# Two of the four weight sums of a seven-product pair formed by an accumulating DMA, with the signs moved to the token side

## The reference

```python
def rms_norm(x, g):
    xf = x.astype(F32)
    y = xf * lax.rsqrt(jnp.mean(xf * xf, axis=-1, keepdims=True) + EPS)
    return (y * g.astype(F32)).astype(x.dtype)

def swiglu(x, w_gate, w_up, w_down):
    return (jax.nn.silu(x @ w_gate) * (x @ w_up)) @ w_down

def reference(...):
    for i in range(DEPTH):            # DEPTH = 4, D_MODEL = 1024, D_FF = 2816, SEQ = 256
        x = x + 0.5 * swiglu(rms_norm(x, norm_g[i, 0]), ffn_w_gate[i, 0], ffn_w_up[i, 0], ffn_w_down[i, 0])
        ...
        x = x + mix @ w_o[i]
        x = x + 0.5 * swiglu(rms_norm(x, norm_g[i, 2]), ffn_w_gate[i, 1], ffn_w_up[i, 1], ffn_w_down[i, 1])
    return rms_norm(x, final_g)
```

## Time and profile before

| | |
|---|---|
| median of 3 runs | 1889.07 us (1888.85 to 1890.01) |
| profiled execution, first to last instruction | 1886.6 us |
| its mean granted PE clock | 0.999 |
| busy, PE / PEld / DVE / ACT / POOL | 99% / 84% / 81% / 57% / 1% |
| DMA moved | 350 MB, 186 GB/s mean |
| chunk loads, all by SP but the first | 303 into `raw`, 24 into `extra` |

### The profile page before, as it was taken

How to read it: one execution, slowest core, us unless ns; L and a number is a source line. 1 busy time by engine, 2 the same in 40 slices (tenths; PEclk the granted TensorE clock), 3 DMA queues, 4 the chain that set the end, 5 groups by cost and what they waited for, 6 DMA issues and landing times.

```text
span 1886.6 us, 22455 instructions
## 1 busy us (share of the span) xinstructions
PE 1873.3 (99%) x9364; PEld 1585.2 (84%) x9364; DVE 1531.9 (81%) x1311; ACT 1074.2 (57%) x1108; POOL 19.9 (1%) x34
## 2 busy tenths in 40 slices
PE   9999999999999999999999999999999999999998
PEld 8888998888888898788888888988888888998886
DVE  7987568987898778898789875689879987569985
ACT  6655555656565544565556554465556654556653
POOL 0000000000000000100000000000000000000000
PEclk9999999999999999999999999999999999999999
DMA  6557343456254643445625454434473545533542
GB/s 249 201 231 267 135 157 134 201 201 243 94 225 197 245 157 112 156 201 201 252 103 225 197 226 158 178 112 201 201 267 126 225 197 188 184 129 137 228 196 87
DMA packets 50052, 350.13 MB, mean 186 GB/s; under 512 B 6168, under 2 KB 6432, under 8 KB 7968
## 3 DMA queue, kind: packets, MB, share of 16 engines
q1 hardware_dynamic: 49360, 346.54, 47.5%
q10 hardware_dynamic: 592, 2.17, 0.3%
HBM read 347.63 MB, written 1.06 MB: 185 GB/s over the span
## 4 chain that ended last, share of the span: by engine, by line
PE 90%; DVE 7%; ACT 2%; issue 1%; POOL 0%; POOLq 0%; ACTq 0%; DVEq 0%
PE work L1261 18%; PE work L1263 18%; PE work L1262 18%; PE acc L1261 10%; PE acc L1263 10%; PE acc L1262 10%; DVE w_lo L756 3%; PE work L1419 1%; PE acc L1305 1%; PE work L1463 1%; PE work L1597 1%; ACT w_hi L465 1%; PE work L1563 0%; PE work L1341 0%; PE work L1567 0%
## 5 line engine op out<-in xcount | busy, mean ns | idle before, releaser
L756 DVE TENSOR_TENSOR w_lo<-raw,w_hi 128x2048 fp32r<-128x2048 f32 x327 | 741.4, 2283 | 33.5 <-ACT w_hi L465 33.4
L465 ACT ACTIVATE w_hi<-raw 128x2048 fp32r<-128x2048 f32 x327 | 613.9, 1909 | 83.2 <-DVE raw L776 64.2
L1261 PE MATMUL work<-w_hi,xg 128*128 128x512 f32 x1040 | 409.6, 394 | 1.0 <-DVE xg L1186 1.0
L1263 PE MATMUL work<-w_hi,xg 128*128 128x512 f32 x1040 | 405.5, 390 | 0.0
L1262 PE MATMUL work<-w_lo,xg 128*128 128x512 f32 x1040 | 405.0, 389 | 0.0
L1261 PE MATMUL acc<-w_hi,m_hi 128*128 128x512 f32 x824 | 325.5, 395 | 0.2
L1263 PE MATMUL acc<-w_hi,m_lo 128*128 128x512 f32 x824 | 321.2, 390 | 0.0
L1262 PE MATMUL acc<-w_lo,m_hi 128*128 128x512 f32 x824 | 320.7, 389 | 0.0
L1263 PEld LDWEIGHTS work<-w_hi,xg 128*128 128x128 f32 x1040 | 195.2, 188 | 41.1
L1261 PEld LDWEIGHTS work<-w_hi,xg 128*128 128x128 f32 x1040 | 195.3, 188 | 40.4 <-issue 1.2
L1262 PEld LDWEIGHTS work<-w_lo,xg 128*128 128x128 f32 x1040 | 195.4, 188 | 38.9
(11 more groups left out here) (200 smaller groups left out, 2169.5 us busy)
## 6 DMA issues: line engine op xcount, KB each, us to landing
raw<-stream_dram SPq DMA_DIRECT2D x303, 1024.0 KB, 5.0
extra<-stream_dram SPq DMA_DIRECT2D x24, 1024.0 KB, 6.9
x<-x_dram SPq DMA_DIRECT2D x2, 512.0 KB, 7.8
raw<-stream_dram ACTq DMA_DIRECT2D x2, 512.0 KB, 7.5
scratch<-cum_rows ACTq DMA_DIRECT2D x1, 1024.0 KB, 5.9
cst<-consts_dram SPq DMA_DIRECT2D x1, 832.0 KB, 6.4
out_dram<-x SPq DMA_DIRECT2D x3, 256.0 KB, 2.4
final_gain<-final_gain_dram SPq DMA_DIRECT2D x1, 512.0 KB, 6.9
```

What stands on the lines that cost most here:

```text
L465: nc.scalar.activation(w_hi[:, c % RING, :], raw_at(place), ACT.Copy).then_inc(hi_ready, 1)
L756: nc.vector.tensor_tensor(w_lo[:, c % RING, :], raw_at(place), w_hi[:, c % RING, :].bitcast(F32), ALU.subtract).then_inc(lo_ready, 1)
L1261: nc.tensor.matmul(dst, a_hi, b_hi, start=start, stop=False, skip_group_check=skip)
L1263: return nc.tensor.matmul(dst, a_lo, b_hi, start=False, stop=stop, skip_group_check=skip)
```

## The change

b11 is read from HBM a second time, into SUMS, behind b22. POOL, when that load has landed, issues a DMA that adds b12 from HBM onto it: SUMS then holds t1 = b11 + b12. A second DMA of POOL adds b22 from HBM onto b12's place in `raw`: t3 = b12 + b22. DVE forms t2 = b11 + t3 and t4 = b21 + t2 as before, but t2 now waits for the second of these DMAs (`t3_added`), and ACT's rounding of t1 for the first (`t1_added`). So that the products still add up, two token sums change sign (S1 = x3 - x1, and S2 and S4 follow by operations with a factor of -1), and the two hidden halves that carry the sign use a negated factor `r_neg`, one more small POOL operation for each block. Each block's six DMAs of POOL stand in POOL's list right behind that.

```diff
-FORMS = "t1", "t3", "t2", "t4"
+FORMS = "t2", "t4"
+ADDED = "t1", "t3"
...
+                loads.append(("b11", layer, n % 3, j, SUMS,
+                              ("top", no * len(PLAIN) + 1) if earlier < 0 else
+                              ("lo", c0 + order.index(("t4", SEVEN[earlier])) + 1)))
...
+            def weight_sums(no):
+
+                for p in range(no * len(SEVEN), (no + 1) * len(SEVEN)):
+                    pool.wait_ge(sums_loaded, 16 * (p + 1))
+                    pool.dma_start(raw_at(SUMS), stream[ADD_FROM[0][p]], accum_op=ALU.add).then_inc(t1_added, 16)
+                    place, count = ADD_ONTO[1][p][3:]
+                    pool.wait_ge(raw_loaded[place], 16 * count)
+                    pool.dma_start(raw_at(place), stream[ADD_FROM[1][p]], accum_op=ALU.add).then_inc(t3_added, 16)
...
+                if n % 3 != 1:
+                    pool.wait_ge(r_col_ready, n + 1)
+                    nc.gpsimd.tensor_tensor(r_neg[:], r_col[:], minus[:], ALU.mult).then_inc(r_neg_ready, 1)
+                    weight_sums(n // 3 * 2 + n % 3 // 2)
...
-                if what in FORMS:
+                if what in ADDED:
+                    act.wait_ge(t1_added if what == "t1" else t3_added, 16 * (no * len(SEVEN) + SEVEN.index(j) + 1))
+                elif what in FORMS:
...
-                if what == "t1":
-                    if j == SEVEN[0]:
-                        dve.wait_ge(top_used, no * len(PLAIN) + 1)
-                    dve.wait_ge(raw_loaded[place["t3"]], 16 * USES[q + PAIR_ORDER.index("t3")][4])
-                    ins = nc.vector.tensor_tensor(raw_at(SUMS), b12, b11, ALU.subtract)
-                elif what == "t3":
-                    dve.wait_ge(b22_loaded, 16 * (p + 1))
-                    ins = nc.vector.tensor_tensor(b12, b22, b12, ALU.subtract)
-                elif what == "t2":
-                    dve.wait_ge(form_ready, len(FORMS) * p + 2)
+                b11, t3, b21 = (raw_at(place[part]) for part in ("b11", "t3", "b21"))
+                if what == "t2":
+                    dve.wait_ge(t3_added, 16 * (p + 1))
                     dve.wait_ge(lo_ready, q + 1)
-                    ins = nc.vector.tensor_tensor(b11, b12, b11, ALU.add)
+                    ins = nc.vector.tensor_tensor(b11, t3, b11, ALU.add)
                 else:
-                    dve.wait_ge(form_ready, len(FORMS) * p + 3)
+                    dve.wait_ge(form_ready, len(FORMS) * p + 1)
                     dve.wait_ge(lo_ready, q + PAIR_ORDER.index("t1") + 1)
-                    ins = nc.vector.tensor_tensor(raw_at(SUMS), b21, b11, ALU.subtract)
+                    ins = nc.vector.tensor_tensor(raw_at(SUMS), b21, b11, ALU.add)
...
-                nc.vector.tensor_tensor(token_sum(S1), token_sum(1), token_sum(3), ALU.add).then_inc(token_sums_ready, 1)
+                nc.vector.tensor_tensor(token_sum(S1), token_sum(3), token_sum(1), ALU.subtract).then_inc(token_sums_ready, 1)
```

More of the change, by code:

```diff
@@ L134, in plan @@
             if what in ("t1", "t4"):
-                uses.append((what, no, j, SUMS, None))
+                uses.append((what, no, j, SUMS, p + 1))
             elif what == "t2":
@@ L143, in plan @@
                 uses.append((what, no, j, len(users) % RAW, len(users) // RAW + 1))
-            for load in ("b12",) if what == "t1" else () if what in FORMS or what == "b22" else (what,):
+            for load in ("b12",) if what == "t1" else () if what in (*FORMS, *ADDED, "b22") else (what,):
                 r = len(users)
@@ L154, in plan @@
                               ("lo", c0 + order.index(("b22", SEVEN[earlier])) + 1)))
+                loads.append(("b11", layer, n % 3, j, SUMS,
+                              ("top", no * len(PLAIN) + 1) if earlier < 0 else
+                              ("lo", c0 + order.index(("t4", SEVEN[earlier])) + 1)))
     return uses, loads
 USES, LOADS = plan()
+ADD_FROM = [i for i, load in enumerate(LOADS) if load[0] == "b12"], [i for i, load in enumerate(LOADS) if load[0] == "b22"]
+ADD_ONTO = [use for use in USES if use[0] == "t1"], [use for use in USES if use[0] == "t3"]
 def trunk(nc, stream, x_in, gains, consts, lam_in, subln_in, wf_in, bf_in, final_in, out):
@@ L205, in trunk @@
         half_neg = sb("half_neg", [P, TB])
+        minus = sb("minus", [P, TB])
+        r_neg = sb("r_neg", [P, TB])
         mean_apart = sb("mean_apart", [P, TB])
@@ L243, in trunk @@
         b22_loaded, form_ready = sem("b22_loaded"), sem("form_ready")
+        sums_loaded, t1_added, t3_added = sem("sums_loaded"), sem("t1_added"), sem("t3_added")
+        minus_ready, r_neg_ready = sem("minus_ready"), sem("r_neg_ready")
         token_sums_ready, token_hi_ready, token_lo_ready = (
@@ L400, in load @@
                     sp.wait_ge({"lo": lo_ready, "form": form_ready, "top": top_used}[free[0]], free[1])
-                sp.dma_start(raw_at(place), stream[i]).then_inc(b22_loaded if place == EXTRA else raw_loaded[place], 16)
+                done = {EXTRA: b22_loaded, SUMS: sums_loaded}
+                sp.dma_start(raw_at(place), stream[i]).then_inc(done[place] if place in done else raw_loaded[place], 16)
             for half in range(2):
@@ L545, in pair_step @@
                     split_to(q + 7)
-                    pair_silu(1, first_part, 0)
+                    pair_silu(1, first_part, 0, r_col)
                     split_to(q + 9)
-                    pair_silu(2, second_part, 1)
+                    act.wait_ge(r_neg_ready, f + 1)
+                    pair_silu(2, second_part, 1, r_neg)
                     split_to(q + 10)
@@ L553, in pair_step @@
                     split_to(q + 11)
-                    pair_silu(3, first_sum, 0)
+                    pair_silu(3, first_sum, 0, r_neg)
                 for s in range(UNITS):
@@ L893, in plain_step @@
                         hidden_lo(s - 1)
-                    form("t3", q)
                     form("t2", q)
@@ L928, in pair_step @@
                     split_to(q + 11)
-                    hidden_of(s, 4, first_sum, 0)
+                    hidden_of(s, 4, first_sum, 0, r_neg)
                 for s in range(UNITS):
```

23 lines of the change are left out of this document (12 added, 11 removed).

## The result

| | before | after |
|---|---|---|
| median of the runs | 1888.96 us (4 runs, 1888.81 to 1890.01) | 2070.87 us (4 runs, 2069.11 to 2073.51) |
| profiled execution, first to last instruction | 1886.6 us | 2071.5 us |
| its mean granted PE clock | 0.999 | 0.959 |

A forecast was written before the change was run, and what follows sets the result against it. PE, busy 99%, was taken as the bound. Eight blocks losing 17.4 us each (139), plus 1.5 in each of two first pairs, made 142 us; added to 1886.6 this gave 2029, as median 2031 us, range 1905 to 2160.

The forecast's parts named there:

- 0.6 + 2.3 + 2.0 + 10.0: First pair, after the SUMS load lands: POOL's instruction, fixed DMA time, other loads in the way, two accumulations, in us.
- the step of 54.5 us: Time from one pair's form t2 to the next pair's, forecast longer than PE's 47.6 us period by 6.9 us.
- A: Transfer time of one accumulating 1 MiB DMA: taken as 5.0 us, with 2.5 and 7.5 as the ends.
- Rivals 1 and 3: 1: accumulation at nearly a load's rate, 1908 to 1960 us, chance 0.22; 3: new chain hidden, 1887 to 1889, chance 0.10.
- Rival 2: Slower DMAs from POOL (A of 7.5 or more, or POOL held by DVE): chance 0.25 for all above 2100 us.
- the sum of 142 us: Forecast total loss: 17.4 us in each of eight blocks, 139, plus 1.5 in each of two first pairs.
- 17.4 as forecast: Lateness of form t2 in a block's third pair, in us, taken as what each block loses.
- the lead: How much later form t2 could start without holding PE: 1.5, 7.2 and 7.5 us in the three pairs.
- the DMA engines' total is not what binds: Over a period between pairs, DMA work of 35.8 us in 54.5, share about 0.65; full only at A = 10.9.
- wrong altogether: Stated signs of failure: PE's waits are for another line, or its granted clock, 1.00 before, falls because of the pauses.

The follow-up runs named there:

- e1: Changed kernel with both of POOL's DMAs per pair as plain copies instead of accumulations, sums not formed: 1920.63 us.
- e2: Changed kernel with each accumulating DMA adding only the first half of the columns, the other half left without its sums: 1933.11 us.
- e5: Changed kernel with only t3 made by accumulating DMA; DVE forms t1 again, no second load of b11: 1944.85 us.
- e6: Changed kernel with only t1 made by accumulating DMA; DVE forms t3: 1935.01 us.
- e8: Changed kernel with ACT's Silu ahead of its rounding of t1, and DVE's `gated` ahead of form t2: 2042.44 us.
- e4: Changed kernel with 16 useless matmuls ahead of PE's wait for `gated` in every second and third pair: 2054.86 us.
- e9: Changed kernel without b22's load for its own product in second and third pairs, part of the result left out: 2022.58 us.
- e7: Changed kernel with b22's load moved behind b21, so b11's second load goes ahead of it: 2059.63 us.

## Why the prediction was right, and what it mis-sized

**Right: what bounds, and the mechanism.** PE was the bound, so 107 us less of DVE bought nothing. Form t2's wait starts a chain of form t2, form t4, SP's loads, POOL and the second accumulation, and that was longer than PE's period: 55.05 us, 54.5 forecast. In the first pair both landings came 15.3 us after POOL's first issue (345.94 to 361.27); the forecast had 0.6 + 2.3 + 2.0 + 10.0 = 14.9. The lateness grew from pair to pair. Taking the accumulation's bytes away (e1, e2) cuts the growth from 7.4 us a step to between 1.5 and 2.4, and with one accumulation alone (e5, e6) PE is hardly later in the third pair than in the second.

**Partly luck: the step of 54.5 us.** Two errors in it nearly cancel. From form t2 to b12's issue it took 28.3 us (361.30 to 389.61), as forecast. But POOL issued 39.95 us after form t2 in the second pair and 39.0 in the third, where the forecast had the load into SUMS landed after 38.0. From there to t3's landing it took 15.05 and 16.0 us, where the forecast had 16.5. In the second pair the load into SUMS landed 3.8 us behind b22's (400.97 against 397.20) and not 2.5, in the third 2.5 (455.07 against 452.59); what makes this difference stays open.

**Right: A.** The forecast took 5.0 us out of 2.5 to 7.5. The two landings lie 4.9 us apart, and 5.5 us of all engines' time by the queue's share. The copy gives 2.45, so the factor is 2.0. That is where the Trainium skill (Collectives: The Full Stack, "The bandwidth ceiling: the fold count and why AG ≠ RS ≠ AR") has a reducing transfer, at half the rate of a copy, and the trace agrees.

**Rivals 1 and 3 fell.** A was not near the load's, and nothing was hidden. Rival 2's large A fell as well.

**Rival 2: POOL was not held.** Its first issues took this, in all 24 pairs (shortest, median, longest, in ns):

```profile
L451 POOL DMA_DIRECT2D extra<-stream_dram x24: 862/865/1025, 33.6 to 1989.9; - x24
```

In the first pair of the second block the issue at 345.94 took 0.90 us although a DVE split ran from 345.89 to 348.17. By the Trainium skill (SBUF — State Buffer, "Who interferes with whom") a DVE operation with two SBUF inputs leaves free the write side that preparing descriptors needs, which the page calls inferred, and this fits. `r_neg`, a POOL operation that reads SBUF, did take 2.16 us at 338.23, beside a DVE split from 338.04, where the forecast had 0.55; it is hidden all the same, as forecast.

**What was mis-sized: the sum of 142 us, which was 184.9.** It left out the clock (put at 1.00), had PE's wait in the wrong place, and had form t2 come too early. What a block loses, taken from the end of b11's products of one block to that of the next, was 30.1, 23.3, 20.5, 25.6, 21.0, 23.2, 20.3 and 20.6 us, 184.6 in all, where the forecast had 17.4 (18.9 in the first and fourth). The second block's 23.3 us can be taken apart:

- 17.4 as forecast.
- 2.2 from the chain: the first form t2 came 1.1 us later than forecast (at 361.30, with PE 30.4 us behind the trace of before, so at 330.9 where 329.8 was forecast), and two steps 0.55 us each.
- 0.9 from the place of PE's wait. The forecast had PE stop at t1's products, the deadline for form t2 being 373.7. In fact `gated`, right behind form t2 on DVE, releases PE one quarter earlier, ahead of b11's products (375.9 in the trace before). `gated` ends 3.1 us after form t2 starts, so form t2's deadline is 372.8. I had read the lead only at the split of t1, the third instruction behind form t2, and not at the two in between. e8 confirms the place: with `gated` first, PE's wait moved to where the forecast had it. Its 28 us are more than eight times 0.9, since there t1's split follows form t2 at once and the steps are shorter.
- 2.7 from the clock, which the forecast took as 1.00 throughout.

That makes 23.2. In the first pairs a second wait of PE, for t1's split, adds up to 1.6 us, 11.0 in all. The first and fourth block lost more, 30.1 and 25.6. There form t2 of the first pair came later: at 49.01 with PE 0.3 us behind, where it stood at 38.67 before, and at 878.00 with PE 74.1 us behind, where it stood at 795.06, which makes 10.0 and 8.8 us against 6.3 in the second block. The first block's first step was 58.5 us as well. That is most of the difference; why the accumulations landed later there stays open.

**Where the clock enters, and where not.** A mean clock of 0.959 over 2071.5 us, with two levels, is 2 x 0.041 x 2071.5 = 170 us at the lower one. PE is 57 us longer busy. Of this only some counts: a slow quarter (12 matmuls) after the first or second pause of a block is made up for by a shorter pause next, as the chain and not PE sets when that ends; behind the third it is lost. There PE's delay against the trace of before grew from 50.96 to 53.66 us, 2.7, and stayed. Eight times 2.7 is 22 us; e4 got back 16.

**The statement that failed: "the DMA engines' total is not what binds".** The share over a period was foretold well: 0.67 from 375.91 to 430.96, against 0.65. But a mean over a period says little of the stretch in it that stands on the path. There the engines were 0.92 and then 0.90 busy, up to the landing for which form t2 waits; afterwards, from 419.48 to 426.31, they were idle (0.00). e9 shows that they bind there, with a step 2.5 to 3.0 us shorter for one load less, and e7 that order helps little (11 us). The kernel before showed 0.86 there already, in a stretch that the forecast did not read. The forecast's sum escaped the error only because it queued the loads one behind the other, 2.5 us each.

**What the profile was to show.** PE's waits in the three pairs of the second block were 4.0 (2.85 and 1.17), 6.11 and 4.37 us, against 3.7, 6.9 and 6.8 forecast: less than forecast in the later ones, since the slow quarters ate into the pauses. "PE waiting for the split of t1 24 times" was wrong in the line and right in the number of pauses. The DMAs took longer than stated, 10.4 and 14.8 us from issue to landing (medians) against about 7.3 and near 13; those two figures left out the other loads in the way. Of what the forecast named as making it "wrong altogether", both came true: PE's waits are for another line (L878), and its granted clock fell. The chain and the growth held all the same, but a good part of the missing 40 us lies in these two.

## What to carry to other kernels

Moving work from an engine that isn't the bound to the DMA engines can win back no more than the bound engine's waits for it, and it costs time as soon as the transfer lands too late for the instruction that needs the value. Compare the length of the new loop (value needed, buffer freed, load, accumulate) with the bound engine's period, since an excess there is paid once per turn, and not once. Read the DMA share in the stretch that ends with the awaited landing, not over the period, and check every instruction queued behind the new wait for who needs it first. Where the bound engine starts to pause, its clock may fall too, so look at the granted clock before pricing the pause by its length alone.

## What the runs showed of the hardware

- **Accumulating DMA.** 1 MiB of float32 from HBM added onto SBUF took 4.9 us from one landing to the next, where a copy took 2.45; half of it, 512 KB, made the step nearly as long as a copy of 1 MiB (50.0 and 49.1 us against 49.4 and 49.3). POOL spent 0.86 us in the first issue of a pair with accumulation and 0.53 without.
- **The granted clock.** In the second block, PE's first matmuls behind a pause of 6.11 us ran at a granted clock of 0.56 over 6.83 us, and then at 1.00. Behind a pause of 1.64 us (e4) it was 1.00 at once. All 16 pauses ahead of second and third pairs in the kernel after (4.3 to 8.8 us) had a stretch at the lower level behind them; two of 1.50 and 1.63 us with four small matmuls between them (ending at 564.77 and 567.06) had none. Over the whole execution 170 us were at the lower level, 5 us in the trace before.
- **More matmuls, less time.** Sixteen useless matmuls ahead of each of 16 pauses made the kernel 16 us faster, though it remained far slower than before.
